# Building the gate matrices of a retrieval layer from three bf16 parts instead of two scaled fp16 parts

## The chip, the cores and the metric

The kernel runs on one core of one Trainium2 chip. The metric is device microseconds (us) of one execution. Before the change it takes 2091.34 us, the median of three runs (2091.04 to 2091.83).

Engine names below are those of the profile: PE is the matrix engine, PEld its weight loads, DVE the vector engine, ACT the scalar engine, POOL the GpSimd engine, SP the engine that issues the transfers.

## The reference, cut to what matters

The layer is a token mixer (pooling, windowed attention and cross-attention, gated and merged), followed by a product-key retrieval over 16,384 single-neuron experts, and a final normalisation. Only the retrieval is touched:

```
q = (hf @ w_q).reshape(T, 8 heads, 2, 128)
s_top, i_top = top_k(q . sub_keys, 16)          # per half: 16 of 128 keys
s_fin, pos = top_k(all 16 x 16 sums, 16)        # 16 experts for each token and head
ids = i_top[first half] * 128 + i_top[second half]
gates = softmax(s_fin)
y = sum over the 128 chosen experts: gate * gelu(x . expert_u[id]) * expert_v[id]
```

T is 512 tokens and the model width is 1024. An expert number is a pair (i, j) of numbers below 128.

## The kernel before, in words

**How the retrieval is computed.** The kernel gathers nothing. It computes all 16,384 activations for all 512 tokens, multiplies them by a gate matrix that is zero where an expert was not chosen, and multiplies the product by all expert values. The experts are cut into 128 blocks of 128: block i holds the experts (i, 0) to (i, 127).

**The stream.** All weights come as 430 chunks of 128x1024 f32, four in flight (`raw`). Each chunk is split in two: ACT rounds it to `w_hi` (line 771), POOL subtracts to get `w_lo` (line 421), and PE multiplies in three passes, high by high, high by low and low by high. `product` (line 442) is one chunk: eight pieces of the contraction times three passes, so 24 matmuls of 512 columns, all at line 448. Both `w_hi` and `w_lo` have two buffers.

**The first matrix product of the retrieval** is 128 such products, one for each block (`experts`, line 698), in three stretches of PE's program: 48 plain ones (`I_PLAIN`), 64 with gate work between them (`I_GATES`), 16 plain ones. ACT applies the gelu from the bank (line 969), and the result is stored to memory (`a_rows`).

**The gate stage** is the stretch of 64, and the change is in it. In each of its 64 steps PE first does the 24 matmuls of one block of experts, and then builds the gate matrices of 8 tokens (`TOK_I`). The gate matrix of a token is 128x128, entry (j, i), and is the product of two matrices with the token's 128 chosen experts (8 heads of 16) along the contraction: `ohJ` has a one where the expert's j is, `ohI` has the expert's gate where its i is. DVE builds both. For each step (`one_hots`, line 1333) it compares a ramp with the i numbers (`eqI`, line 1339), waits until PE is done with the buffer (line 1341), compares the ramp with the j numbers (`ohJ`, line 1342), and multiplies `eqI` by the gates (`ohI`, line 1345). Each of these works on 128x1024 elements of 16 bits. `ohJ`, `eqI` and `ohI` have two buffers each, so DVE may be up to two steps ahead of PE.

**How a gate is carried in 16 bits.** The gates are multiplied by 2^15 (`GATE_SCALE`), rounded to fp16, and the rest is rounded to fp16 again: two parts (`GATE_PARTS`). So `ohI` is made twice, and PE does two matmuls of 128 columns for each token, 16 in a step (line 729), into two banks, four tokens in each. ACT reads the banks back, multiplies by 2^-15 and writes `gstage` (line 993), which is stored to memory (`g_rows`, line 301).

**What sets the order.** Each engine's program is written out by hand and runs in order; semaphores join them. In the gate stage PE waits for `lo_ready` (POOL's half of the chunk), `proj_read` (ACT's gelu), `gate_read` (ACT's reading of the gate banks) and `hot_ready` (DVE's matrices). DVE waits for `gate_mm` (PE's gate matmuls two steps back). ACT waits for `chunk_used` and `gate_mm`; POOL waits for `hi_ready`, which ACT gives.

**Before the gate stage**, DVE finds the top experts, PE turns their i, j and gates so that experts lie on partitions (line 713), and DVE widens them into `I2`, `J2` and `G2` (lines 1320 to 1327). **After it** come the 16 plain blocks and then the value stage, which loads both stored matrices again, multiplies them on DVE (line 1364) and on PE by the expert values (line 645).

Of the kernel before, what the change touches and what calls it, by code (L numbers as in the profile page):

```python
# [18 lines left out]
T, D, P = 512, 1024, 128  # L19
# [6 lines left out]
PEER_H, TOPK, NKEYS = 8, 16, 128  # L26
# [25 lines left out]
TOK_I = T // I_GATES  # L52
# [4 lines left out]
SMALLS = 6  # L57
QUARTERED = 28
AHEAD = 6
GATE_PARTS, GATE_SCALE = 2, 2.0 ** 15  # L60


def build(nc, dram, out):
    f32, f32r, f16, u32, i32 = (mybir.dt.float32, mybir.dt.float32r, mybir.dt.float16,
                                mybir.dt.uint32, mybir.dt.int32)
    ACT, ALU, AX = mybir.ActivationFunctionType, mybir.AluOpType, mybir.AxisListType

    with ExitStack() as ctx:
# [6 lines left out]
        class Place:  # L75
# [2 lines left out]
                self.at = at  # L78

            def __call__(self, name, shape, dt=f32):  # L80
                size = int(np.prod(shape)) * (2 if dt == f16 else 4)
                line = 512 if size % 512 == 0 else 64
                at = (arena_at + self.at + line - 1) // line * line
                t = nc.alloc_sbuf_tensor_at(name, [P] + list(shape), dt, offset=at)
                self.at = at - arena_at + size
                assert self.at <= arena_size, (name, self.at)
                return t

        keep = Place(0)
# [9 lines left out]
        pscale = keep("pscale", [4])  # L99
        sinks = keep("sinks", [16])  # L100
        freq = keep("freq", [2])
        iota_b = keep("iota_b", [NKEYS], f16)
        iota_k = keep("iota_k", [TOPK])
        eps = keep("eps", [1])
        ssum = keep("ssum", [8])
# [52 lines left out]
        r = Place(front)  # L158
# [4 lines left out]
        GT = r("GT", [T])  # L163
        R1 = r("R1", [T])
        gsm = r("gsm", [TT * PEER_H])
        I2 = r("I2", [T, 2], f16)
        J2 = r("J2", [T, 2], f16)
        G2 = r("G2", [GATE_PARTS, T, 2], f16)
        eqI = r("eqI", [2, TOK_I, NKEYS], f16)
        ohJ = r("ohJ", [2, TOK_I, NKEYS], f16)  # L170
        ohI = r("ohI", [2, GATE_PARTS, TOK_I, NKEYS], f16)
        late = r.at
        sc = r("sc", [TT, 2 * PEER_H, NKEYS])
        cand = r("cand", [PEER_H, TOPK * TOPK])
# [22 lines left out]
        bank = [ctx.enter_context(nc.psum_tensor(f"bank{b}", [P, 512], f32)) for b in range(8)]  # L197
# [5 lines left out]
        def sem(name):  # L203
            return ctx.enter_context(nc.semaphore(name))
# [28 lines left out]
        spread, spread_read = sem("spread"), sem("spread_read")  # L233
        hot_ready, gate_mm, gate_read = sem("hot_ready"), sem("gate_mm"), sem("gate_read")
# [201 lines left out]
        def _(pe):  # L436
# [60 lines left out]
            for q in range(4):  # L497
                chunk(S_VM + q)
                for k in range(2):
                    for m in range(MT):  # L500
                        for low_m, w in ((0, w_hi), (0, w_lo), (1, w_hi)):
                            last = pe.matmul(bank[2 + m][:, :], memT[low_m][:, 2 * q + k, m * P:(m + 1) * P],
                                             w[:, q % 2, k * T:(k + 1) * T],
                                             start=(q == 0 and k == 0 and low_m == 0 and w is w_hi),
                                             stop=(q == 3 and k == 1 and low_m == 1))
# [78 lines left out]
            for u in range(8):  # L584
# [4 lines left out]
                for n in range(TT):  # L589
                    for h in range(2):  # L590
# [3 lines left out]
                                         start=True, stop=True)  # L594
# [7 lines left out]
            for u in range(4):  # L602
# [3 lines left out]
                for n in range(TT):  # L606
                    last = pe.matmul(mem_scores(u, n), qr[:, u % 2, n * P:(n + 1) * P], kmT[:, u, :],
                                     start=True, stop=True)
# [89 lines left out]
            def experts(i0, di):  # L698

                n, rn = S_U + di, R_U + di  # L700
                chunk(n + i0)
                pe.wait_ge(proj_read, rn - 1 + i0)
                product(bank[rn % 2][:, :], n % 2, hT)
# [14 lines left out]
            with pe.Fori(0, I_GATES - 2 + 1, 2) as i0:  # L718
                for di in range(2):
                    experts(i0 + I_PLAIN, di)  # L720
                    for b in range(2):

                        pe.wait_ge(gate_read, i0 * 2 + (2 * di + b + 1))
                        if b == 0:
                            pe.wait_ge(hot_ready, i0 + (di + 1))
                        for tk in range(TOK_I // 2):
                            at = b * (TOK_I // 2) + tk
                            for q in range(GATE_PARTS):
                                last = pe.matmul(bank[2 + b][:, tk * P:(tk + 1) * P], ohJ[:, di, at, :],  # L729
                                                 ohI[:, di, q, at, :], start=(q == 0), stop=(q == GATE_PARTS - 1))  # L730
                        last.then_inc(gate_mm, 1)
            with pe.Fori(I_PLAIN + I_GATES, NI - 1, 2) as i0:
                for di in range(2):
# [25 lines left out]
        def _(act):  # L759
            step = Steps(act, act_step)  # L760
# [25 lines left out]
            for k in range(KC):  # L786
                act.wait_ge(turned, k + 1)
                act.activation(memT_hi[:, k, :], bank[k][:, 0:M], ACT.Copy,
                               scale=gains[:, 1, k:k + 1]).then_inc(turned_hi, 1)
# [172 lines left out]
            def gelu(i0, di):  # L962
                base = S_U + di
                split(base + 2, loop=i0)
                act.wait_ge(chunk_used, base + 1 + i0)

                if not (isinstance(i0, int) and i0 + di < 2):
                    act.wait_ge(a_stored[di % 2], (i0 + (di - di % 2)) * 8)
                act.activation(abuf[:, di % 2, :], bank[(R_U + di) % 2][:, :],  # L969
                               ACT.Gelu_apprx_tanh).then_inc(proj_read, 1)  # L970
# [12 lines left out]
            def gates_out(i0, first=False):  # L983
                for half in range(2):
                    if not first:
                        act.wait_ge(g_stored[half], i0 * (4 * 16 // (2 * PER)))
                    for k in range(PER):
                        di = half * PER + k
                        gelu(i0 + I_PLAIN, di)
                        for b in range(2):  # L990
                            act.wait_ge(gate_mm, i0 * 2 + (2 * di + b + 1))
                            t0 = k * TOK_I + b * TOK_I // 2
                            act.activation(gstage[:, half, :, t0:t0 + TOK_I // 2].rearrange("p i t -> p t i"),  # L993
                                           bank[2 + b][:, :].rearrange("p (t i) -> p t i", i=NKEYS),
                                           ACT.Copy, scale=1.0 / GATE_SCALE).then_inc(gate_read, 1)

            gates_out(0, first=True)
            with act.Fori(2 * PER, I_GATES - 2 * PER + 1, 2 * PER) as i0:
                gates_out(i0)
# [30 lines left out]
        def _(dve):  # L1030
            step = Steps(dve, dve_step)
# [285 lines left out]
            def pairs(src):  # L1317
                return src.unsqueeze(2).broadcast_to([P, T, 2])

            dve.tensor_copy(I2[:, :, :], pairs(bank[2][:, :]))  # L1320
            dve.tensor_copy(J2[:, :, :], pairs(bank[3][:, :]))
            dve.tensor_scalar(G2[:, 0, :, :], pairs(bank[4][:, :]), GATE_SCALE, None, ALU.mult)
            dve.tensor_scalar(GT[:, :], bank[4][:, :], GATE_SCALE, None, ALU.mult).then_inc(spread_read, 1)
            dve.wait_ge(spread_read, 1)

            step(dve.tensor_tensor(R1[:, :], GT[:, :], G2[:, 0, :, 0], ALU.subtract))
            step(dve.tensor_copy(G2[:, 1, :, :], pairs(R1[:, :])))

            keys = [P, TOK_I, NKEYS // 2, 2]
            ramp = iota_b[:, :].rearrange("p (n e) -> p n e", e=2).unsqueeze(1).broadcast_to(keys)  # L1330
# [2 lines left out]
            def one_hots(i0, di, first=False):  # L1333
                toks = bass.ds(i0 * TOK_I + di * TOK_I, TOK_I)

                def over_keys(src):
                    return src.unsqueeze(2).broadcast_to(keys)

                dve.tensor_tensor(eqI[:, di, :, :].rearrange(wide, e=2), ramp, over_keys(I2[:, toks, :]), ALU.is_equal)
                if not first:  # L1340
                    dve.wait_ge(gate_mm, i0 * 2 + (2 * di - 2))
                dve.tensor_tensor(ohJ[:, di, :, :].rearrange(wide, e=2), ramp, over_keys(J2[:, toks, :]), ALU.is_equal)  # L1342
                dve.drain()
                for q in range(GATE_PARTS):
                    last = dve.tensor_tensor(ohI[:, di, q, :, :].rearrange(wide, e=2),  # L1345
                                             eqI[:, di, :, :].rearrange(wide, e=2),
                                             over_keys(G2[:, q, toks, :]), ALU.mult)
                last.then_inc(hot_ready, 1)

            for di in range(2):  # L1350
                one_hots(0, di, first=True)
            with dve.Fori(2, I_GATES - 2 + 1, 2) as i0:
                for di in range(2):
                    one_hots(i0, di)
# [110 lines left out]
```

## Time and profile before

| what | value |
|---|---|
| median of three runs | 2091.34 us |
| the profiled execution | 2091.04 us |
| its span, first to last instruction | 2088.5 us |
| PE busy | 2041.2 us, 98% of the span |
| PE weight loads busy | 1680.6 us, 80% |
| DVE busy | 1169.3 us, 56% |
| ACT busy | 791.9 us, 38% |
| POOL busy | 893.0 us, 43% |
| transfers | 323.46 MB, 155 GB/s over the span |

The span is what the profiler sees between the first and the last instruction; the 2.5 us between it and the execution's time lie outside the engines' programs. A row of the timeline gives a start in us from the start of the span, a duration, and in brackets the idle time of the engine ahead of it with what ended that idle time.

### The profile page before, as it was taken

The page shows a single profiled execution, that of the slowest core. Times are in us where ns is not written, and L with a number is a line of the kernel's source. Part 1 is how long each engine was busy: PE and PEld are TensorE (multiplying, and loading weights), DVE is VectorE, ACT ScalarE, POOL GpSimd, SP SyncE. Part 2 cuts the span into 40 slices and gives each one's busy share as a digit, 9 for nine tenths or more (in the row PEclk, how much of TensorE's full clock was granted, in tenths as well). Part 3 has the DMA queues.
Part 4 walks back from the last instruction along what each step waited for, and adds up shares of the span by engine and source line. Part 5 has one row for each costly group of instructions (what it writes and reads, how often), then busy time and mean ns, then how long its engine had stood idle before and what let it go on. Part 6 is the DMA issues. An engine that isn't in the chain of part 4 may idle for free.

```text
span 2088.5 us, 29235 instructions
## 1 busy us (share of the span) xinstructions
PE 2041.2 (98%) x10104; PEld 1680.6 (80%) x10104; DVE 1169.3 (56%) x1785; ACT 791.9 (38%) x1136; POOL 893.0 (43%) x445
## 2 busy tenths in 40 slices
PE   7989999999999999999999999999999999999998
PEld 6767788887888888888888888888888888888886
DVE  5677222222129999777777774035555555555556
ACT  5477423223222222355555554222223232232323
POOL 6522144443335444444444444444444444444443
PEclk9999999999999999999999999999999999999999
DMA  5211122222224445446666666764555555555552
GB/s 222 86 37 41 51 91 100 94 97 81 80 81 136 150 136 151 138 128 204 203 201 201 201 201 202 239 247 181 189 198 211 181 185 188 201 208 180 186 189 97
DMA packets 108515, 323.46 MB, mean 155 GB/s; under 512 B 11200, under 2 KB 11200, under 8 KB 106304
## 3 DMA queue, kind: packets, MB, share of 16 engines
q1 hardware_dynamic: 108192, 322.49, 45.9%
q10 hardware_dynamic: 288, 0.54, 0.1%
q8 instruction: 18, 0.29, 0.1%
q14 instruction: 17, 0.14, 0.0%
HBM read 253.78 MB, written 69.21 MB: 155 GB/s over the span
## 4 chain that ended last, share of the span: by engine, by line
issue 44%; PE 32%; POOL 22%; DMA 0%; POOLq 0%; DVE 0%; ACT 0%; SPq 0%
PE bank L645 32%; POOL w_lo L421 22%; DMA a_in<-a_rows 0%; POOLq L418 0%; DVE x_sb L1390 0%; POOLq L428 0%; DVE x_sb L1385 0%; DVE wf L1364 0%; POOL mask L405 0%; POOL mask L403 0%; DVE wT_lo L1368 0%; ACT wT_hi L1002 0%; POOL mask L400 0%; POOLq L425 0%; POOL mask L408 0%
## 5 line engine op out<-in xcount | busy, mean ns | idle before, releaser
L421 POOL TENSOR_TENSOR w_lo<-raw,w_hi 128x1024 fp32r<-128x1024 f32 (+1 forms) x430 | 889.4, 2076 | 1176.8 <-ACT w_hi L771 1176.8
L771 ACT ACTIVATE w_hi<-raw 128x1024 fp32r<-128x1024 f32 x346 | 366.7, 1060 | 1194.1 <-PE bank L448 673.8
L448 PE MATMUL bank<-hT_hi,w_hi 128*128 128x512 f32 x1488 | 591.5, 397 | 0.5 <-POOL w_lo L421 0.4
L448 PE MATMUL bank<-hT_hi,w_lo 128*128 128x512 f32 x1488 | 580.8, 390 | 0.0
L448 PE MATMUL bank<-hT_lo,w_hi 128*128 128x512 f32 x1488 | 579.6, 390 | 0.0
L1368 DVE TENSOR_TENSOR wT_lo<-wf,wT_hi 128x512 fp32r<-128x512 f32 x128 | 313.0, 2445 | 130.7 <-ACT wT_hi L1002 130.7
L448 PEld LDWEIGHTS bank<-hT_hi,w_lo 128*128 128x128 f32 x1488 | 279.5, 188 | 59.8
L448 PEld LDWEIGHTS bank<-hT_hi,w_hi 128*128 128x128 f32 x1488 | 280.0, 188 | 59.0 <-issue 4.0
L448 PEld LDWEIGHTS bank<-hT_lo,w_hi 128*128 128x128 f32 x1488 | 280.3, 188 | 56.1 <-issue 0.7
L645 PE MATMUL bank<-w_hi,wT_hi 128*128 128x512 f32 x1024 | 315.5, 389 | 0.1
L645 PE MATMUL bank<-w_lo,wT_hi 128*128 128x512 f32 x1024 | 315.4, 389 | 0.0
L645 PE MATMUL bank<-w_hi,wT_lo 128*128 128x512 f32 x1024 | 315.4, 389 | 0.0
L1364 DVE TENSOR_TENSOR wf<-a_in,g_in 128x512 f32<-128x512 f32 x128 | 88.9, 694 | 253.3 <-PE bank L645 159.5
L645 PEld LDWEIGHTS bank<-w_hi,wT_hi 128*128 128x128 f32 x1024 | 192.2, 188 | 40.3 <-DVE wT_lo L1368 0.5
L645 PEld LDWEIGHTS bank<-w_lo,wT_hi 128*128 128x128 f32 x1024 | 192.3, 188 | 39.9
L645 PEld LDWEIGHTS bank<-w_hi,wT_lo 128*128 128x128 f32 x1024 | 192.3, 188 | 39.8
L1345 DVE TENSOR_TENSOR ohI<-eqI,G 128x1024 f16<-128x1024 f16 x128 | 209.9, 1678 | 9.2
L993 ACT ACTIVATE gstage<-bank 128x512 f32<-128x512 f32 x128 | 129.7, 1123 | 0.0
L1213 DVE TENSOR_TENSOR part<-sg,bank 128x512 f32<-128x512 f32 x24 | 15.1, 683 | 171.8 <-PE bank L448 171.8
L1342 DVE TENSOR_TENSOR ohJ<-iota_b,J 128x1024 f16<-128x1024 f16 x64 | 44.3, 692 | 107.3 <-PE bank L729 107.3
L1002 ACT ACTIVATE wT_hi<-wf 128x512 fp32r<-128x512 f32 x128 | 78.6, 614 | 3.4 <-DVE wf L1364 3.2
L969 ACT ACTIVATE abuf<-bank 128x512 f32<-128x512 f32 x128 | 74.2, 580 | 1.6 <-DMA a_rows<-abuf 1.6
(215 smaller groups left out, 1462.9 us busy)
## 6 DMA issues: line engine op xcount, KB each, us to landing
raw<-stream SPq DMA_DIRECT2D x346, 512.0 KB, 3.5
a_rows<-abuf SPq DMA_DIRECT2D x128, 256.0 KB, 4.0
g_rows<-gstage SPq DMA_DIRECT2D x32, 1024.0 KB, 6.1
g_in<-g_rows SPq DMA_DIRECT2D x16, 2048.0 KB, 9.1
a_in<-a_rows SPq DMA_DIRECT2D x128, 256.0 KB, 3.5
x_sb<-x SPq DMA_DIRECT2D x4, 512.0 KB, 8.5
out<-x_sb SPq DMA_DIRECT2D x4, 512.0 KB, 2.6
subkeys<-subkeys SPq DMA_DIRECT2D x1, 1024.0 KB, 14.5
```

The source lines that it names most:

```text
L421: last = pool.tensor_tensor(w_lo[:, k % 2, cols], raw[:, k % RAW, cols], w_hi[:, k % 2, cols].bitcast(f32), ALU.subtract)
L448: last = pe.matmul(dst, w[:, slot, k * P:(k + 1) * P], rhs[low][:, r0 + k - k0, :], start=(k == k0 and wi == 0), stop=(k == k1 - 1 and wi ...
L645: last = pe.matmul(bank[2 * t + half][:, :], lhs[low_l][:, t * P:(t + 1) * P], w[:, slot, half * 512:(half + 1) * 512], start=first and lo ...
L771: act.activation(w_hi[:, base % 2, :], raw[:, slot, :], ACT.Copy).then_inc(hi_ready, 1)
L969: act.activation(abuf[:, di % 2, :], bank[(R_U + di) % 2][:, :], ACT.Gelu_apprx_tanh).then_inc(proj_read, 1)
L993: act.activation(gstage[:, half, :, t0:t0 + TOK_I // 2].rearrange("p i t -> p t i"), bank[2 + b][:, :].rearrange("p (t i) -> p t i", i=NKEYS),
L1002: act.activation(wT_hi[:, di % 2, :], wf[:, di % 2, :], ACT.Copy).then_inc(weighted_hi, 1)
L1213: dve.tensor_tensor(part[:, q, :], sg[:, q, :], bank[b][:, :], ALU.mult).then_inc(branch_read, 1)
L1342: dve.tensor_tensor(ohJ[:, di, :, :].rearrange(wide, e=2), ramp, over_keys(J2[:, toks, :]), ALU.is_equal)
L1345: last = dve.tensor_tensor(ohI[:, di, q, :, :].rearrange(wide, e=2), eqI[:, di, :, :].rearrange(wide, e=2), over_keys(G2[:, q, toks, :]), ...
L1364: dve.tensor_tensor(wf[:, di % 2, :].rearrange(tiles, b=BLOCKS), a_in[:, di % 4, :].rearrange(tiles, b=BLOCKS), g_in[:, di // GROUP, :, di ...
L1368: dve.tensor_tensor(wT_lo[:, di % 2, :], wf[:, di % 2, :], wT_hi[:, di % 2, :].bitcast(f32), ALU.subtract).then_inc(weighted_lo, 1)
```

## The change

The two scaled fp16 parts become three bf16 parts without a scale. All 16-bit tiles (`iota_b`, `I2`, `J2`, `G2`, `eqI`, `ohJ`, `ohI`) become bf16. The numbers in the comparisons are below 128, which both types hold exactly.

```
-GATE_PARTS, GATE_SCALE = 2, 2.0 ** 15
-        G2 = r("G2", [GATE_PARTS, T, 2], f16)
+        G2 = r("G2", [3, T, 2], bf16)
-        ohI = r("ohI", [2, GATE_PARTS, TOK_I, NKEYS], f16)
+        ohI = r("ohI", [2, 3, TOK_I, NKEYS], bf16)
...
-                            for q in range(GATE_PARTS):
+                            for q in range(3):
                                 last = pe.matmul(bank[2 + b][:, tk * P:(tk + 1) * P], ohJ[:, di, at, :],
-                                                 ohI[:, di, q, at, :], start=(q == 0), stop=(q == GATE_PARTS - 1))
+                                                 ohI[:, di, q, at, :], start=(q == 0), stop=(q == 2))
...
-                                           ACT.Copy, scale=1.0 / GATE_SCALE).then_inc(gate_read, 1)
+                                           ACT.Copy).then_inc(gate_read, 1)
...
-            dve.tensor_scalar(G2[:, 0, :, :], pairs(bank[4][:, :]), GATE_SCALE, None, ALU.mult)
-            dve.tensor_scalar(GT[:, :], bank[4][:, :], GATE_SCALE, None, ALU.mult).then_inc(spread_read, 1)
+            dve.tensor_copy(G2[:, 0, :, :], pairs(bank[4][:, :]))
+            dve.tensor_copy(GT[:, :], bank[4][:, :]).then_inc(spread_read, 1)
...
             step(dve.tensor_copy(G2[:, 1, :, :], pairs(R1[:, :])))
+            step(dve.tensor_tensor(GT[:, :], R1[:, :], G2[:, 1, :, 0], ALU.subtract))
+            step(dve.tensor_copy(G2[:, 2, :, :], pairs(GT[:, :])))
...
-                for q in range(GATE_PARTS):
+                for q in range(3):
                     last = dve.tensor_tensor(ohI[:, di, q, :, :].rearrange(wide, e=2),
```

In the changed program every line after 60 has a number that is one lower, up to the added DVE lines, and one higher after them. PE, in one step of the gate stage, before (bank2 and bank3 are the two gate banks, `ohI` the moving and `ohJ` the stationary operand; the first rows are the end of a block of experts):

```order
L448 MATMUL bank0<-hT_hi_50,w_lo_54 128x512
L723 ISA
L725 REGISTER_ALU [waits gate_read]
L729 MATMUL bank2<-ohI_118,ohJ_117 128x128 [waits hot_ready]
L729 MATMUL bank2<-ohI_118,ohJ_117 128x128 x7
L723 REGISTER_ALU
L729 MATMUL bank3<-ohI_118,ohJ_117 128x128 [waits gate_read]
L729 MATMUL bank3<-ohI_118,ohJ_117 128x128 x7
```

And the same place in the changed program:

```order
L447 MATMUL bank0<-hT_hi_50,w_lo_54 128x512
L722 ISA
L724 REGISTER_ALU [waits gate_read]
L728 MATMUL bank2<-ohI_118,ohJ_117 128x128 [waits hot_ready]
L728 MATMUL bank2<-ohI_118,ohJ_117 128x128 x11
L722 REGISTER_ALU
L728 MATMUL bank3<-ohI_118,ohJ_117 128x128 [waits gate_read]
L728 MATMUL bank3<-ohI_118,ohJ_117 128x128 x11
```

Each bank gets 12 matmuls where it had 8; the waits stand where they stood.

DVE, from the widening of the gates to the first matrices and the first step of the loop, before (`G_115` is `G2`, `R_111` is `R1`):

```order
L1322 TENSOR_SCALAR G_115<-bank 128x1024
L1323 TENSOR_SCALAR GT<-bank 128x512
L1326 TENSOR_TENSOR R_111<-GT,G_115 128x512 [waits spread_read]
L1327 CAST G_115<-R_111 128x1024 [waits dve_step]
L1339 TENSOR_TENSOR eqI<-iota_b,I_113 128x1024 [waits dve_step]
L1342 TENSOR_TENSOR ohJ<-iota_b,J_114 128x1024
L1345 TENSOR_TENSOR ohI<-eqI,G_115 128x1024 x2
```

And the same place in the changed program:

```order
L1321 CAST G_115<-bank 128x1024
L1322 COPY GT<-bank 128x512
L1325 TENSOR_TENSOR R_111<-GT,G_115 128x512 [waits spread_read]
L1326 CAST G_115<-R_111 128x1024 [waits dve_step]
L1327 TENSOR_TENSOR GT<-R_111,G_115 128x512 [waits dve_step]
L1328 CAST G_115<-GT 128x1024 [waits dve_step]
L1340 TENSOR_TENSOR eqI<-iota_b,I_113 128x1024 [waits dve_step]
L1343 TENSOR_TENSOR ohJ<-iota_b,J_114 128x1024
L1346 TENSOR_TENSOR ohI<-eqI,G_115 128x1024 x3
```

Two DVE instructions are added once, and one `ohI` multiplication in every step. The instructions of ACT, POOL and SP keep their order and number.

## Rows read from the trace of the kernel before

**Rows 1.** Busy time of each engine in the gate stage, one window.

```profile
core 0: us, PE busy (x) PEld busy (x) DVE busy (x) ACT busy (x) POOL busy (x), PEclk, DMA share, GB/s
887.50:1300.15 412.65, 412.65 (x2562) 338.60 (x2562) 282.71 (x247) 221.88 (x256) 179.14 (x64) 1.00 0.60 194
```

**Rows 2.** The waits of three engines in the gate stage, 885 to 1300 us.

```profile
engine line waited for: us in total, times, longest us
POOL w_lo L421 <- ACT w_hi L771: 235.4, 65, 4.0
ACT w_hi L771 <- PE bank L448: 191.6, 64, 3.9
DVE ohJ L1342 <- PE bank L729: 107.3, 62, 1.7
```

**Rows 3.** Timeline of PE, around two gate bursts, one step apart.

```profile
1003.56 1.07 PE L729 MATMUL bank<-ohI,ohJ 128*128 128x128 f16 x16
1004.44 0.47 PE L448 MATMUL bank<-hT_hi,w_hi 128*128 128x512 f32 x1
1004.75 0.39 PE L448 MATMUL bank<-hT_lo,w_hi 128*128 128x512 f32 x1
...
1010.01 1.07 PE L729 MATMUL bank<-ohI,ohJ 128*128 128x128 f16 x16
```

**Rows 4.** Timeline of ACT, two plain steps ahead of the gate stage.

```profile
848.27 1.06 ACT L771 ACTIVATE w_hi<-raw 128x1024 fp32r<-128x1024 f32 x1 [3.94 <-PE bank L448]
853.71 1.06 ACT L771 ACTIVATE w_hi<-raw 128x1024 fp32r<-128x1024 f32 x1 [3.90 <-PE bank L448]
```

**Rows 5.** The gate matmuls and their weight loads, min/median/max ns, first and last start; one burst's loads.

```profile
L729 PEld LDWEIGHTS bank<-ohI,ohJ x1024: 95/98/101, 887.5 to 1294.5; 128*128 128x128 f16 x171
L729 PE MATMUL bank<-ohI,ohJ x1024: 218/219/231, 887.5 to 1294.5; 128*128 128x128 f16 x171
...
1003.56 0.90 PEld L729 LDWEIGHTS bank<-ohI,ohJ 128*128 128x128 f16 x16 [0.26 <-issue]
```

**Rows 6.** Timeline of PE, a burst of f32 matmuls of 128 columns.

```profile
869.84 0.60 PE L713 MATMUL bank<-ident,IF 128*128 128x128 f32 x4
870.27 0.60 PE L713 MATMUL bank<-ident,JF 128*128 128x128 f32 x4
```

**Rows 7.** Timeline of DVE, one step of the gate stage (and the first of its two `ohI` alone).

```profile
1004.76 0.69 DVE L1342 TENSOR_TENSOR ohJ<-iota_b,J 128x1024 f16<-128x1024 f16 x1 [1.73 <-PE bank L729]
1005.60 3.29 DVE L1345 TENSOR_TENSOR ohI<-eqI,G 128x1024 f16<-128x1024 f16 x2
1005.60 2.68 DVE L1345 TENSOR_TENSOR ohI<-eqI,G 128x1024 f16<-128x1024 f16 x1
1008.80 0.68 DVE L1339 TENSOR_TENSOR eqI<-iota_b,I 128x1024 f16<-128x1024 f16 x1
```

**Rows 8.** Timeline of POOL, one with DVE resting beside it, one in the gate stage.

```profile
860.29 2.40 POOL L421 TENSOR_TENSOR w_lo<-raw,w_hi 128x1024 fp32r<-128x1024 f32 x1 [3.04 <-ACT w_hi L771]
1004.89 2.84 POOL L421 TENSOR_TENSOR w_lo<-raw,w_hi 128x1024 fp32r<-128x1024 f32 x1 [3.61 <-ACT w_hi L771]
```

**Rows 9.** Timeline of ACT, one step of the gate stage.

```profile
1003.76 1.06 ACT L771 ACTIVATE w_hi<-raw 128x1024 fp32r<-128x1024 f32 x1 [2.97 <-PE bank L448]
1005.20 2.02 ACT L993 ACTIVATE gstage<-bank 128x512 f32<-128x512 f32 x2
```

**Rows 10.** Timeline of DVE ahead of the gate stage.

```profile
873.62 1.21 DVE L1322 TENSOR_SCALAR G<-bank 128x1024 f16<-128x1024 f32 x1
875.47 0.69 DVE L1326 TENSOR_TENSOR R<-GT,G 128x512 f32<-128x512 f32 x1
876.19 0.69 DVE L1327 CAST G<-R 128x1024 f16<-128x1024 f32 x1
880.94 0.68 DVE L1345 TENSOR_TENSOR ohI<-eqI,G 128x1024 f16<-128x1024 f16 x1
886.35 0.68 DVE L1339 TENSOR_TENSOR eqI<-iota_b,I 128x1024 f16<-128x1024 f16 x1
```

More of the change, by code:

```diff
@@ L59 @@
 AHEAD = 6
-GATE_PARTS, GATE_SCALE = 2, 2.0 ** 15
 def build(nc, dram, out):
-    f32, f32r, f16, u32, i32 = (mybir.dt.float32, mybir.dt.float32r, mybir.dt.float16,
-                                mybir.dt.uint32, mybir.dt.int32)
+    f32, f32r, bf16, u32, i32 = (mybir.dt.float32, mybir.dt.float32r, mybir.dt.bfloat16,
+                                 mybir.dt.uint32, mybir.dt.int32)
     ACT, ALU, AX = mybir.ActivationFunctionType, mybir.AluOpType, mybir.AxisListType
@@ L80, in __call__ @@
             def __call__(self, name, shape, dt=f32):
-                size = int(np.prod(shape)) * (2 if dt == f16 else 4)
+                size = int(np.prod(shape)) * (2 if dt == bf16 else 4)
                 line = 512 if size % 512 == 0 else 64
@@ L101, in build @@
         freq = keep("freq", [2])
-        iota_b = keep("iota_b", [NKEYS], f16)
+        iota_b = keep("iota_b", [NKEYS], bf16)
         iota_k = keep("iota_k", [TOPK])
@@ L165, in build @@
         gsm = r("gsm", [TT * PEER_H])
-        I2 = r("I2", [T, 2], f16)
-        J2 = r("J2", [T, 2], f16)
-        G2 = r("G2", [GATE_PARTS, T, 2], f16)
-        eqI = r("eqI", [2, TOK_I, NKEYS], f16)
-        ohJ = r("ohJ", [2, TOK_I, NKEYS], f16)
-        ohI = r("ohI", [2, GATE_PARTS, TOK_I, NKEYS], f16)
+        I2 = r("I2", [T, 2], bf16)
+        J2 = r("J2", [T, 2], bf16)
+        G2 = r("G2", [3, T, 2], bf16)
+        eqI = r("eqI", [2, TOK_I, NKEYS], bf16)
+        ohJ = r("ohJ", [2, TOK_I, NKEYS], bf16)
+        ohI = r("ohI", [2, 3, TOK_I, NKEYS], bf16)
         late = r.at
```

## The prediction
> **What bounds the kernel now.** I read the page first (PE busy 98% of the span), then the busy time of the gate stage, which is all the change touches. There PE is busy for all 412.65 us, at a granted clock of 1.00, which is the 2.4 GHz level, while DVE works 282.71, ACT 221.88 and POOL 179.14 [rows 1]. The list of waits says the same from the other side: POOL waits for ACT, ACT waits for PE, DVE waits for PE, and PE waits for nobody [rows 2]. So PE sets the pace of the stage, and the reader should see DVE as an engine that rests 1.73 us in each step of 6.45 us until PE gives it back a buffer [rows 3, 7].
>
> One step, from burst to burst, is 1010.01 - 1003.56 = 6.45 us [rows 3]. A plain step without gate work is 853.71 - 848.27 = 5.44 us [rows 4], 24 matmuls at 0.227 us. The gate burst of 16 matmuls thus costs 1.01 us of PE's time in each of the 64 steps. Nothing ahead of PE hides any of it.
>
> **The change part by part.**
>
> *PE: 8 more matmuls of 128 columns in each of 64 steps, 512 in all.* They stand in one row with the 16 that are there, behind the same waits. What does one cost? The trace gives four readings, and they lie close together. From the first gate matmul to the first matmul of the next block, 1004.44 - 1003.56 = 0.88 us for 16 [rows 3]: 55.0 ns. The burst's own row spans 1.07 us and one matmul takes 0.219 [rows 3, 5], so 15 starts in 0.85 us: 56.7 ns. The burst's weight loads span 0.90 us at 0.098 each [rows 5]: 53.5 ns. And the whole excess of a step, 1.01 us over 16: 63 ns; this is the upper end, because it also holds what is paid once in a step and not for each matmul, such as the 0.31 us between the first two f32 matmuls behind the burst where the others take 0.227 [rows 3, 4]. I take 56 ns, between the two readings from matmul starts: 8 x 0.056 = 0.448 us in a step, 64 x 0.448 = 28.7 us. The ends are 512 x 0.0535 = 27.4 us and 512 x 0.063 = 32.3 us.
>
> That bf16 costs what fp16 costs is not shown by a row of bf16, as there is none. But a column takes 0.227/512 = 0.443 ns in the f32 passes of the product [rows 4] and 0.056/128 = 0.438 ns in the fp16 burst: in this kernel even a change of width does not change the time of a column. Each matmul loads its own stationary matrix, also where the one before used the same one (1024 loads for 1024 matmuls [rows 5]), and at 53.5 ns from start to start the loads keep up with matmuls at 56 ns. Eight more of either do not alter that.
>
> The Trainium skill, "TensorE: Matmul & The Clock Gate", section "Wait — 56ns, not 53.3ns?", has a matmul of 128 columns start every 55.6 ns at the full clock. By that figure, as an estimate, the term would be 28.5 us; the row's 55.0 and 56.7 ns lie around it.
>
> *DVE: one more `ohI` multiplication a step.* Two of them take 3.29 us, the first alone 2.68 [rows 7]. The first is long because POOL's subtraction runs beside it from 1004.89 to 1007.73 [rows 8]; it ends 0.55 us after POOL, and the second adds 3.29 - 2.68 = 0.61. Without POOL beside it one takes 0.68 [rows 10]. So the third costs 0.6 us if it runs behind POOL's, which it does: the first ends at 1008.28, POOL ended at 1007.73. DVE's chain in a step is from 1004.76 to 1009.48, 4.72 us [rows 7]; it becomes 5.3 us, in a step of 6.45 + 0.45 = 6.90 us. DVE still rests 1.6 us, and it is a step ahead of PE at that. Cost: nothing, hidden behind PE's products. If the third were also held up by POOL (2.0 us more) the chain would be 7.3 us, 0.4 over the step, or 26 us more in 64 steps; that needs a second POOL instruction inside one step, and there is one only. At the other end there is nothing to gain on DVE.
>
> One detail will move. DVE's `ohJ` waits for the end of the burst, which comes 0.45 us later, at about 1005.20 in the times of this step. POOL's subtraction is released by ACT's `w_hi`, which waits for the product and not for the burst [rows 9], and starts at 1004.89. So POOL will start first, and `ohJ` rather than the first `ohI` will be the long one: it ends 0.55 us after POOL, at about 7.84 instead of 5.45, the three `ohI` follow at about 8.0, 8.6 and 9.2, `eqI` ends at 10.5, and the next release comes at 12.1. DVE rests the same 1.6 us. POOL then should take 2.40 us as it does beside a resting DVE, not 2.84 [rows 8]. PE needs its result only when the next product is done, some 3 us after 1007.73, so neither change is worth anything.
>
> The Trainium skill, "SBUF — State Buffer", section "Who interferes with whom", says that a DVE instruction with two SBUF inputs and a GpSimd instruction that reads SBUF exclude each other, and that whoever starts first holds the port to the end. By that rule `ohJ` (start 1004.76) held up POOL and POOL held up `ohI`, as the trace has it, and the exchange just described follows. It also speaks against this change: five DVE instructions back to back can keep POOL out. By the same rows the most that POOL can lose is one DVE instruction, 0.69 us of its 3 us of cover, so the time would be the same.
>
> *DVE, once:* the two scaled conversions become plain ones, at the same element counts (1.21 us for the wide one [rows 10]); added are one subtraction and one conversion of the sorts that take 0.69 us each, 0.72 from start to start [rows 10]. With the third `ohI` the first step's matrices are ready at 881.62 + 1.44 + 0.60 = 883.7 us; PE's first burst starts at 887.5 [rows 5]. The second step's, ready at 886.4 before, come at 889.1 for a burst at about 894.4. Covered, with 3.8 and 5.3 us to spare; even a hold-up of 2.4 us by POOL fits.
>
> *ACT:* `gstage` loses its scale and keeps size and count, 2.02 us for two, ending at 1007.22, and PE's next burst is at 1010.01 [rows 3, 9]. The banks are full 0.45 us later and there are still over 2 us. Cost nothing.
>
> *SP, transfers, POOL:* same instructions, same bytes; each step is 0.45 us longer, so they have more room. The larger tiles move others in SBUF by 6 KB a partition, which has no price in any row.
>
> *Sum.* 2091.04 us for the profiled execution + 28.7 = 2119.7 us. The median before is 0.3 us above that execution, so the expected median is 2120.0 us. Single steps: 5.44 us plain, 6.90 us with gates.
>
> **The rivals.**
>
> A, *the added matmuls cost more than those before* (a longer burst drains what feeds PE). For it: the burst is the fastest run of instructions in the program, a load and a matmul every 56 ns against 227 in the product. Against: 16 pairs show no slowing, and every burst is alike (matmuls 218 to 231 ns [rows 5]). Its price, if the extra ones went at the pace of f32 matmuls of 128 columns, 0.43/4 = 108 ns [rows 6]: 512 x 0.108 = 55 us, 2146 us; anything between 2124 and that belongs to it.
>
> B, *DVE becomes the bound.* The mechanism: the bf16 instructions don't run at the 0.68 us of the fp16 ones but at the pace of a conversion of 1024 elements from the banks, 1.21 us [rows 10]. Then a step is 5 x 1.21 + 2.0 (POOL) + 0.15 = 8.2 us, against 6.90: 64 x 1.3 = 83 us on top, 2203 us. It decides from 0.95 us for each instruction (5 x 0.95 + 2.15 = 6.90). For it: the trace has no bf16 row. Against: same width, same shapes, and fp16 at 0.68 us where 512 f32 elements take 0.69 [rows 10], so what counts there is the bytes.
>
> C, *not slower: bf16 matmuls are faster than fp16 ones.* Place: the burst. 24 of them would have to fit in the 0.88 us of the 16, so 36.7 ns each; from there on the kernel is no slower, and the time stays at 2091 us. Against: both types of the kernel take 0.44 ns for a column. For it: only that no bf16 row exists. The other way to the same end, that the burst falls into idle time of PE, is excluded by the stage's PE busy time [rows 1]. A part of it would be the 0.26 us by which the weight loads rest ahead of each burst [rows 5]; if the third part let that vanish, the kernel would gain 16.6 us back, 2103 us, but the matmuls themselves show no gap there.
>
> **How the numbers follow.** The forecast, PE pays 53.5 to 63 ns for each of 512 matmuls and nothing else shows: 0.91. A: 0.04. B: 0.03. C: 0.02, half of it the case at 2103 us, which is still faster than the forecast but slower than before. The forecast's own range is 2118.7 to 2123.6; with 0.4 us for the scatter of the runs it is 2118.2 to 2124.0, and more than 9 in 10 fall there, so it needs no stretching to the other cases. 0.2% is 4.2 us, about what a measurement of this kernel tells from no change. Slower: forecast, A, B and half of C, 0.99; within it: 0.008; faster 0.002.
>
> **What the profile after would show.** Right: bursts of x24 about 1.5 us long, with the next f32 matmul 1.33 us behind the first of the burst; bursts 6.90 us apart; PE busy throughout, no wait of PE on DVE; DVE waiting 1.6 us a step at `ohJ`; a long `ohJ` (2.6 us), short `ohI` and POOL at 2.4 us. The stages ahead of 887.5 us and behind the gate stage keep their lengths. Wrong: PE waiting for `hot_ready` (B), bursts apart by more than 6.97 us with a gap inside them (A), or less than 6.87 us (C).

## The result, and the profile after

The changed kernel takes 2123.37 us, the median of four timed executions (2119.13 to 2125.07), against 2091.28 us (2091.04 to 2091.83) for the kernel before: a ratio of 1.0146, 95% interval 1.0128 to 1.0165. Forecast were 2120.0 us and 2118.2 to 2124.0. All its ten executions lie between 2118.74 and 2128.57 us, a scatter that the kernel before did not show at first. One execution of the kernel before, run beside the later experiments, took 3440.47 us at a mean granted clock of 0.556 and is left out everywhere below. The profiled execution took 2123.92 us, with a span of 2121.9.

What answers to [rows 1] and [rows 2] is one window of the gate stage from its first burst on (columns as in rows 1), and the waits in it:

```profile
892.27:1333.40 441.13, 441.13 (x3073) 367.00 (x3073) 321.25 (x313) 221.91 (x256) 154.04 (x64) 1.00 0.56 182
```

```profile
POOL w_lo L420 <- ACT w_hi L770: 292.8, 66, 4.5
ACT w_hi L770 <- PE bank L447: 223.6, 65, 3.9
DVE ohJ L1343 <- PE bank L728: 96.5, 61, 1.6
PEld bank L728 <- issue: 16.7, 64, 0.3
```

PE is busy throughout at a granted clock of 1.00, waits for nobody, and the others wait for it. A step of PE, the answer to [rows 3], and all gate matmuls, the answer to [rows 5]:

```profile
1009.46 1.51 PE L728 MATMUL bank<-ohI,ohJ 128*128 128x128 bf16 x24
1010.78 0.47 PE L447 MATMUL bank<-hT_hi,w_hi 128*128 128x512 f32 x1
1011.09 0.39 PE L447 MATMUL bank<-hT_lo,w_hi 128*128 128x512 f32 x1
```

```profile
L728 PEld LDWEIGHTS bank<-ohI,ohJ x1536: 96/98/100, 892.3 to 1327.8; 128*128 128x128 bf16 x192
L728 PE MATMUL bank<-ohI,ohJ x1536: 219/219/230, 892.3 to 1327.8; 128*128 128x128 bf16 x192
```

The next matmul starts 1.32 us behind the first of the burst, where it was 0.88, and still takes 0.47 us with 0.31 to the one after it: what is paid once in a step has not grown. The next burst starts at 1016.35 us, so a step is 6.89 us, where 6.90 were forecast. From the first gate matmul to the last are 435.5 us, and 407.0 before: 28.5 us for 512 more matmuls (504 in 63 steps and 8 in the last burst), 55.7 ns each. With the first starts, 887.5 and 892.3, and the spans the whole difference falls in three parts: 4.8 us ahead of the gate stage, 28.5 in it, 0.1 behind it (2121.9 - 1327.8 = 794.1; 2088.5 - 1294.5 = 794.0).

DVE and POOL in a step, the answers to [rows 7] and [rows 8]:

```profile
1011.10 2.63 DVE L1343 TENSOR_TENSOR ohJ<-iota_b,J 128x1024 bf16<-128x1024 bf16 x1 [1.61 <-PE bank L728]
1013.88 1.89 DVE L1346 TENSOR_TENSOR ohI<-eqI,G 128x1024 bf16<-128x1024 bf16 x3
1015.69 0.68 DVE L1340 TENSOR_TENSOR eqI<-iota_b,I 128x1024 bf16<-128x1024 bf16 x1
```

```profile
1010.79 2.40 POOL L420 TENSOR_TENSOR w_lo<-raw,w_hi 128x1024 fp32r<-128x1024 f32 x1 [4.49 <-ACT w_hi L770]
```

The exchange is there: POOL now starts 0.31 us ahead of `ohJ` and takes 2.40 us, `ohJ` takes 2.63, the three `ohI` 1.89 together, and DVE rests 1.61 us.

The 4.8 us ahead of the gate stage were not foreseen. They are what is left of a delay that arises in the windowed attention, between 120 and 220 us, in code that the change does not touch. The last scaling of that stage starts 7.9 us later than before (214.3 and 206.4 us). Part of it is won back further on: by the lines of the kernel before, DVE's first instruction of line 1213 starts 6.0 us later (276.7 and 270.7), ACT's first of line 960 4.7 us later (527.4 and 522.7). In the attention stage DVE scales the probabilities in eight rounds of eight short instructions, and in each round POOL subtracts a chunk in four pieces. The first round takes 4.07 us in both traces. The second to fourth, before:

```profile
124.64 2.66 DVE L1182 TENSOR_SCALAR prob<-prob,rinv 128x256 f32<-128x256 f32 x8
137.87 2.19 DVE L1182 TENSOR_SCALAR prob<-prob,rinv 128x256 f32<-128x256 f32 x8
151.16 2.66 DVE L1182 TENSOR_SCALAR prob<-prob,rinv 128x256 f32<-128x256 f32 x8
```

```profile
126.39 2.87 POOL L421 TENSOR_TENSOR w_lo<-raw,w_hi 128x256 fp32r<-128x256 f32 x4 [12.65 <-ACT w_hi L771]
139.67 3.04 POOL L421 TENSOR_TENSOR w_lo<-raw,w_hi 128x256 fp32r<-128x256 f32 x4 [10.41 <-ACT w_hi L771]
152.91 2.87 POOL L421 TENSOR_TENSOR w_lo<-raw,w_hi 128x256 fp32r<-128x256 f32 x4 [10.20 <-ACT w_hi L771]
```

And the same three rounds after:

```profile
125.02 3.14 DVE L1181 TENSOR_SCALAR prob<-prob,rinv 128x256 f32<-128x256 f32 x8
138.65 3.60 DVE L1181 TENSOR_SCALAR prob<-prob,rinv 128x256 f32<-128x256 f32 x8
152.74 4.07 DVE L1181 TENSOR_SCALAR prob<-prob,rinv 128x256 f32<-128x256 f32 x8
```

```profile
126.50 2.92 POOL L420 TENSOR_TENSOR w_lo<-raw,w_hi 128x256 fp32r<-128x256 f32 x4 [12.39 <-ACT w_hi L770]
139.74 3.10 POOL L420 TENSOR_TENSOR w_lo<-raw,w_hi 128x256 fp32r<-128x256 f32 x4 [10.32 <-ACT w_hi L770]
153.29 3.10 POOL L420 TENSOR_TENSOR w_lo<-raw,w_hi 128x256 fp32r<-128x256 f32 x4 [10.45 <-ACT w_hi L770]
```

In the first of these DVE starts 0.38 us later against the start of the span, POOL only 0.11, so DVE's lead on POOL is 1.48 us instead of 1.75. More of the scaling then lies beside POOL's work, and the round takes 0.48 us longer. The lead shrinks to 1.09 and 0.55 us in the next two rounds, which take 3.60 and 4.07 us, and the four behind these take 4.07 to 4.14 us each. Before, the lead stays at 1.75 to 1.80 us up to the seventh round, and a round takes 2.19 or 2.66 us; the rounds are 13.2 to 13.3 us apart there, and 13.6 and 14.1 after.

### The profile page after: what moved, and what is told of

The parts are those of the page before. It is cut to its first block, busy times and chain, and to the rows that moved or that the text cites. A ratio compares the mean times of both kernels' runs of the same rounds, so it can differ in the third digit from the quotient of the medians.

```text
span 2121.9 us, 30387 instructions
## 1 busy us (share of the span) xinstructions
PE 2068.2 (97%) x10616; PEld 1705.7 (80%) x10616; DVE 1217.6 (57%) x1851; ACT 791.6 (37%) x1136; POOL 869.7 (41%) x445
## 4 chain that ended last, share of the span: by engine, by line
issue 46%; PE 32%; POOL 21%; DMA 0%; POOLq 0%; DVE 0%; ACT 0%; SPq 0%
PE bank L644 32%; POOL w_lo L420 21%; DMA a_in<-a_rows 0%; POOLq L417 0%; DVE x_sb L1391 0%; POOLq L427 0%; DVE x_sb L1386 0%; DVE wf L1365 0%; POOL mask L402 0%; POOL mask L404 0%; DVE wT_lo L1369 0%; ACT wT_hi L1001 0%; POOL mask L399 0%; POOLq L424 0%; SPq L267 0%
## 5 line engine op out<-in xcount | busy, mean ns | idle before, releaser
L420 POOL TENSOR_TENSOR w_lo<-raw,w_hi 128x1024 fp32r<-128x1024 f32 (+1 forms) x430 | 866.1, 2022 | 1233.4 <-ACT w_hi L770 1233.4
L1343 DVE TENSOR_TENSOR ohJ<-iota_b,J 128x1024 bf16<-128x1024 bf16 x64 | 164.1, 2565 | 96.5 <-PE bank L728 96.5
L1346 DVE TENSOR_TENSOR ohI<-eqI,G 128x1024 bf16<-128x1024 bf16 x192 | 121.3, 687 | 9.2
L728 PEld LDWEIGHTS bank<-ohI,ohJ 128*128 128x128 bf16 x1536 | 85.9, 98 | 16.7 <-issue 16.7
L728 PE MATMUL bank<-ohI,ohJ 128*128 128x128 bf16 x1536 | 96.9, 219 | 0.0
```

Source lines behind the costliest of these rows:

```text
L420: last = pool.tensor_tensor(w_lo[:, k % 2, cols], raw[:, k % RAW, cols], w_hi[:, k % 2, cols].bitcast(f32), ALU.subtract)
```

## The experiments

Two theories went in. M: the change costs 512 matmuls of 55.4 ns on PE and nothing else, whatever the 16-bit type. R: the rest is the meeting of POOL and DVE in the attention stage, which comes out differently from one execution to the next, in any version. The rivals: T, the type bears part of the cost; D, DVE's third multiplication bears part of it; S, the scatter comes from the start of the program and is only carried along. A reader should know that no long execution of the kernel before was profiled; what its executions above 2096 us hold is read from traces of the variants.

The first four experiments ran on one chip, the last three on another. Beside the first four stood 23 executions of the kernel before, which themselves spread over 2090.99 to 2101.53 us, median 2097.16. So the close agreement of the first four executions of before had been the lower part of a wide spread. A median of four to twelve executions is therefore uncertain by some microseconds, and the length of the gate stage in each trace is the sharper evidence.

**Three fp16 parts (e1).** The kernel before, with the counts of the change.

```
-GATE_PARTS, GATE_SCALE = 2, 2.0 ** 15
+GATE_PARTS, GATE_SCALE = 3, 2.0 ** 15
...
             step(dve.tensor_copy(G2[:, 1, :, :], pairs(R1[:, :])))
+            step(dve.tensor_tensor(GT[:, :], R1[:, :], G2[:, 1, :, 0], ALU.subtract))
+            step(dve.tensor_copy(G2[:, 2, :, :], pairs(GT[:, :])))
```

> The kernel before with three scaled fp16 parts, so the counts of the change without its type. Theory M (the time is the 512 added matmuls at 55.4 ns each, whatever the 16-bit type): gate steps of 6.89 us, the gate stage 28.3 us longer, fastest executions at 2119.1 us as with bf16. Theory T (the type bears part of the cost): steps shorter than 6.89 us and a fastest execution clearly under 2119 us. Theory R (the executions of the changed kernel above 2119 us come from the attention stage, where POOL's and DVE's instructions meet in a different order from one execution to the next): some executions again 3 to 9 us above the fastest, and where the profile is of such a one, the extra time lies between 120 and 220 us of the span and DVE's scaling of the probabilities has a mean over 500 ns instead of 414.

Measured: 2120.16 to 2128.57 us, median 2123.83, ratio 1.0136 (1.0110 to 1.0162). The lowest of the four is 1.1 us above the 2119.1 expected. All gate matmuls:

```profile
L729 PE MATMUL bank<-ohI,ohJ x1536: 219/219/230, 893.5 to 1329.0; 128*128 128x128 f16 x192
```

First to last are 435.5 us, as with bf16. The profiled execution (2125.1 us) is one of the long ones, its first burst 6.0 us later than before, and DVE's scaling, over the whole attention stage, has this row, against 435 ns before (the 414 of the expectation is the mean without the first round):

```profile
L1182 DVE TENSOR_SCALAR prob<-prob,rinv 128x256 f32<-128x256 f32 x64 | 32.6, 581 | 0.3
```

The type bears nothing of the gate stage's cost with three parts.

**Two bf16 parts (e2).** The changed kernel without its third part.

```
-        ohI = r("ohI", [2, 3, TOK_I, NKEYS], bf16)
+        ohI = r("ohI", [2, 2, TOK_I, NKEYS], bf16)
...
-                            for q in range(3):
+                            for q in range(2):
...
-            step(dve.tensor_tensor(GT[:, :], R1[:, :], G2[:, 1, :, 0], ALU.subtract))
-            step(dve.tensor_copy(G2[:, 2, :, :], pairs(GT[:, :])))
```

> The changed kernel with two bf16 parts instead of three; it leaves out the third part of each gate, so the gates are rounded to 16 bits. Theory M: the time of the kernel before, 2091.0 to 2091.8 us in its fast executions, gate steps of 6.45 us, bursts of 16 with the next matmul 0.88 us behind the first. Theory T: between 2091 and 2119, or DVE's 16-bit instructions no longer at 0.68 us. Theory R: nothing in the gate stage, but executions some us above the fastest may occur, as with any program.

Measured: 2090.68 to 2099.41 us, median 2096.91, against 2097.16 for the kernel before beside it: ratio 0.9995 (0.9980 to 1.0010). The gate matmuls and DVE's `ohI`:

```profile
L728 PE MATMUL bank<-ohI,ohJ x1024: 219/219/230, 894.2 to 1301.2; 128*128 128x128 bf16 x171
```

```profile
L1344 DVE TENSOR_TENSOR ohI<-eqI,G 128x1024 bf16<-128x1024 bf16 x128 | 210.0, 1679 | 9.2
```

407.0 us from first to last, and 1679 ns where fp16 had 1678. T falls, from the other side too.

**PE's third matmul alone (e3).**

```
-                            for q in range(GATE_PARTS):
+                            for at_q, q in enumerate((0, 1, 1)):
                                 last = pe.matmul(bank[2 + b][:, tk * P:(tk + 1) * P], ohJ[:, di, at, :],
-                                                 ohI[:, di, q, at, :], start=(q == 0), stop=(q == GATE_PARTS - 1))
+                                                 ohI[:, di, q, at, :], start=(at_q == 0), stop=(at_q == 2))
```

> The kernel before, where PE takes the second fp16 part a second time (it adds that part twice, so the output is off in the last bits of the gates); DVE's work is as before. Theory M: the full 28.3 us, steps of 6.89 us. A rival, that part of the cost comes with DVE's third multiplication or with the larger tiles: less than 28 us here. The order of POOL and DVE in a step should already be exchanged, since it hangs on the end of the burst alone: ohJ about 2.6 us, ohI 0.68, POOL's subtraction 2.40.

Measured: 2119.51 to 2125.66 us, median 2124.30, ratio 1.0133 (1.0108 to 1.0158). DVE and POOL in one step:

```profile
1003.89 2.64 DVE L1342 TENSOR_TENSOR ohJ<-iota_b,J 128x1024 f16<-128x1024 f16 x1 [2.14 <-PE bank L729]
1006.68 1.29 DVE L1345 TENSOR_TENSOR ohI<-eqI,G 128x1024 f16<-128x1024 f16 x2
```

```profile
1003.58 2.41 POOL L421 TENSOR_TENSOR w_lo<-raw,w_hi 128x1024 fp32r<-128x1024 f32 x1 [4.42 <-ACT w_hi L771]
```

The bursts run from 892.0 to 1327.5 us, again 435.5. PE's matmuls alone bring the whole cost in the gate stage, and the later end of the burst alone makes the exchange of POOL and `ohJ`.

**DVE's third multiplication alone (e4).**

```
+        spare = r("spare", [2, TOK_I, NKEYS], f16)
...
+                last = dve.tensor_tensor(spare[:, di, :, :].rearrange(wide, e=2),
+                                         eqI[:, di, :, :].rearrange(wide, e=2),
+                                         over_keys(G2[:, 1, toks, :]), ALU.mult)
                 last.then_inc(hot_ready, 1)
```

> The kernel before, where DVE multiplies a third time into a spare tile that nobody reads; PE's work is as before. Theory M: 2091 us in the fastest executions, steps of 6.45 us, DVE's rest at ohJ down from 1.73 to about 1.1 us. The rival (DVE's third multiplication costs something): above 2092 us in the fastest executions. POOL and DVE keep their order in a step here: ohJ 0.69 us, the first ohI 2.68, POOL 2.84. Theory R: this program has the same PE and POOL programs as before; executions some us above the fastest may still occur, with the extra time between 120 and 220 us.

Measured: 2090.90 to 2099.84 us, median 2095.75, ratio 0.9994 (0.9980 to 1.0008). One step of DVE:

```profile
1003.87 0.69 DVE L1343 TENSOR_TENSOR ohJ<-iota_b,J 128x1024 f16<-128x1024 f16 x1 [1.14 <-PE bank L730]
1004.71 3.28 DVE L1346 TENSOR_TENSOR ohI<-eqI,G 128x1024 f16<-128x1024 f16 x2
1007.91 0.68 DVE L1349 TENSOR_TENSOR spare<-eqI,G 128x1024 f16<-128x1024 f16 x1
```

The rest falls from 1.73 to 1.14 us, by the 0.6 us of the forecast, and the gate stage is 407.0 us long, from 893.1 to 1300.1: the third multiplication costs nothing. D falls. This profiled execution is a long one too, and its second round in the attention stage differs from that of before in another way than the changed kernel's:

```profile
124.76 4.07 DVE L1183 TENSOR_SCALAR prob<-prob,rinv 128x256 f32<-128x256 f32 x8
125.46 2.95 POOL L422 TENSOR_TENSOR w_lo<-raw,w_hi 128x256 fp32r<-128x256 f32 x4 [11.61 <-ACT w_hi L772]
```

DVE starts only 0.12 us later than before, but POOL 0.93 us earlier. What goes with the long course is the lead between the two, here 0.70 us.

**A fourth matmul on PE (e5)**, three times the second part, as above with (0, 1, 1, 1).

> The kernel before, where PE takes the second fp16 part three times (the output is off in the last bits of the gates): 32 matmuls in a burst, 1024 more than before. Theory M, linear in the count: steps of 6.45 + 2 x 0.443 = 7.33 us, 56.7 us more than before, fastest executions at 2147.5 us. The rival, that a longer burst is fed more slowly (the third was cheap, the fourth is not): steps above 7.4 us and a gap inside the burst's row, which should be 1.96 us long.

Measured: 2148.04 to 2157.34 us, median 2152.85, ratio 1.0287 (1.0264 to 1.0310).

```profile
997.52 1.96 PE L729 MATMUL bank<-ohI,ohJ 128*128 128x128 f16 x32
...
1004.86 1.96 PE L729 MATMUL bank<-ohI,ohJ 128*128 128x128 f16 x32
```

Steps are 7.34 us; 6.45, 6.89 and 7.34 us for 16, 24 and 32 matmuls lie on a line of about 56 ns a matmul. (From the first to the last matmul are 464.2 us, 57.2 more than before for 1024 more matmuls: 55.9 ns each.) The burst is fed no more slowly when it doubles. Its profiled execution has the early first burst (887.4 us) and is the lowest time, 2148.04; the forecast was 2147.5.

**Turns in the attention stage (e6).** POOL's subtraction waits in seven of the eight rounds until DVE has scaled the probabilities, first in the kernel before. The edit also writes the last twelve of the 28 quartered subtractions out one by one, which had stood in a loop; no run has this without the wait.

```
-            with pool.Fori(0, QUARTERED - RAW + 1, RAW) as n0:
+            with pool.Fori(0, 16 - RAW + 1, RAW) as n0:
                 for k in range(RAW):
                     low(n0 + k, k, pieces=4)
+            for n in range(16, QUARTERED):
+                if 1 <= n - (S_Q + 3) <= 7:
+                    pool.wait_ge(prob_ready, 4 * (n - (S_Q + 3)))
+                low(n, n % RAW, pieces=4)
```

> The kernel before, where POOL's subtraction for seven chunks of the attention stage waits until DVE has scaled the probabilities of the step before. Theory R (the scatter is the meeting of these two): the scatter goes, all executions within about 1 us, and the level is that of the fastest before or some us lower, 2085 to 2091.5 us; DVE's scaling takes 340 to 360 ns an instruction in all its rows. The rival, that the scatter comes from the start (loads and the clock in the first 50 us) and is only carried along: the executions scatter over 2091 to 2101 us as the kernel before does beside it. A second rival: POOL's later subtraction makes PE wait for its half of the chunk, all executions above 2096 us.

Measured: 2086.57 to 2091.37 us in 12 executions, median 2089.82. Beside it the kernel before took 2091.27 to 2092.31 us nine times and 2096.4 to 2100.74 seven times. Ratio 0.9976 (0.9965 to 0.9987): this version is faster than both kernels. DVE and POOL:

```profile
124.52 2.19 DVE L1186 TENSOR_SCALAR prob<-prob,rinv 128x256 f32<-128x256 f32 x8
137.92 2.19 DVE L1186 TENSOR_SCALAR prob<-prob,rinv 128x256 f32<-128x256 f32 x8
151.16 2.19 DVE L1186 TENSOR_SCALAR prob<-prob,rinv 128x256 f32<-128x256 f32 x8
```

```profile
126.79 2.79 POOL L421 TENSOR_TENSOR w_lo<-raw,w_hi 128x256 fp32r<-128x256 f32 x4 [11.45 <-DVE prob L1186]
```

The upper group of times is gone, as R has it. But the expectation of a scatter within 1 us was wrong: 4.8 us are left. Where they come from is not shown. The eighth round has no wait and still varies (2.67 us in this trace, 3.13 in that of the next run), and other stages were not taken apart. S as the whole cause is excluded by the seven traces without the wait: their first scaling starts between 110.03 and 111.27 us, at most 1.2 us apart, and their first gate burst between 887.4 and 894.2 us.

**The same wait in the changed kernel (e7).**

> The changed kernel with the same wait on POOL. Theories M and R together: the time of the kernel before with that wait plus 28.3 us, within 0.7 us, and as little scatter. If it is apart from that sum by more than 1 us, something of the change outside the gate stage costs time.

Measured: 2117.26 to 2119.39 us, median 2118.64, ratio 1.0118 (1.0099 to 1.0136) to the kernel before. The two medians with turns are 2118.64 - 2089.82 = 28.8 us apart, expected 28.3 within 0.7. The scatter is 2.1 us, where the changed kernel had 9.8. In the two profiled executions the gate stage is 28.7 us longer (885.8 to 1321.4 us, against 887.5 to 1294.4), but starts 1.7 us earlier, so their spans are only 27.0 us apart. The close fit of the medians may therefore owe something to chance.

## Why the prediction was right, and where it was not

**PE sets the pace and pays for every added matmul.** Right. 28.7 us were forecast; the gate stage grew by 28.5. The value of 56 ns was between the readings of 55.0 and 56.7; the runs give 55.7, and 55.9 with a fourth matmul. The upper end of 63 ns rightly held what is paid once in a step. The Trainium skill, "TensorE: Matmul & The Clock Gate", section "Wait — 56ns, not 53.3ns?", states 55.6 ns: the runs agree within 0.3 ns.

**bf16 costs what fp16 does.** Right, on PE (three fp16 parts, two bf16 parts: 435.5 and 407.0 us, as with the other type) and on DVE (1679 against 1678 ns). It had been argued from the time of a column; the two runs show it. The argument itself was weaker than it read. That a change of width leaves the time of a column alone does not hold for every matmul here: those of [rows 6] take 0.43/4 = 108 ns for 128 columns, 0.84 ns a column, at a granted clock of 1.00. And that only the bytes count on DVE does not fit the cast of [rows 10], which takes 0.69 us for 1024 f32 elements, as the subtraction does for 512.

**DVE's third multiplication is hidden.** Right: 0.6 us, as forecast, a rest of 1.61 us a step with the change, and no cost alone.

**The exchange of POOL and `ohJ`.** Right in each number: 2.63, 1.89 and 2.40 us. It costs nothing in the gate stage (28.5 us for 512 matmuls is what the matmuls alone explain), and comes from PE's burst alone. The rule of the Trainium skill, "SBUF — State Buffer", section "Who interferes with whom", that of a DVE and a GpSimd instruction that need the shared port the first to start holds it, foretold who would be slow.

**The matrices ahead of the first burst.** Right:

```profile
883.12 2.76 DVE L1340 TENSOR_TENSOR eqI<-iota_b,I 128x1024 bf16<-128x1024 bf16 x1
886.56 1.89 DVE L1346 TENSOR_TENSOR ohI<-eqI,G 128x1024 bf16<-128x1024 bf16 x3
```

The first `ohI` are done at 886.56 + 1.89 = 888.45 us and the burst starts at 892.3, 3.8 us later, as forecast. POOL did hold up one instruction there (`eqI`, 2.76 us), as was allowed for, while the first long `ohI` of before is gone.

**Rivals A, B and C.** None occurred: a burst of 32 matmuls still takes 1.96 us, without a gap; PE waits for nobody in the gate stage, so DVE was never late; the type brought no gain.

**The step that failed** is one sentence: "The stages ahead of 887.5 us and behind the gate stage keep their lengths." Behind, they did; ahead, the profiled execution lost 4.8 us. The forecast took the three close executions of the kernel before that were known as its spread, and put 0.4 us into the range for it. The true spread of that kernel, seen beside the experiments, is 10.5 us: 16 of 39 executions under 2094 us, 23 from 2096 to 2102. That the median fell in the range owes something to luck: e3, with the same program on PE, had a median of 2124.30 us, just above the range's end of 2124.0, and e1 had 2123.83. The 32.1 us between the two medians of the result are likewise more than the change costs. Compared like with like the forecast is better than the medians make it look: the lowest executions are 2090.99 and 2118.74 us, 27.8 apart, and the medians of the two versions with turns 28.8.

**What stays open:** what sets DVE's lead on POOL in the second round of the attention stage. Up to there the programs of before and after differ only in the type of `iota_b` and in where tiles lie. The changed kernel's instructions start up to 0.9 us earlier between 8 and 36 us, and a steady 0.4 us later from about 49 us on; no run here took the start apart. Whether the first four executions of before all fell in the lower group by chance or by their chip is open too.

## What to carry to other kernels

Where an engine is busy through a whole stage and waits for nobody, the price of another instruction on it is the start-to-start time of its neighbours, and the trace has it; readings that include what is paid once in a step bound it from above. On the engines beside it, count the rest in a step, and ask what the later end of a burst re-orders.

Before a few microseconds are put down to a change, look for where they arise: here 4.8 of 33.4 us lay in code that was not touched, and more executions of the kernel before showed a scatter of that size in it too. A spread in a program of fixed work can come from two engines that meet now earlier and now later. Here making one of them wait was faster than letting both try, by 1.9 us even against the lower group of before (medians 2089.82 and 2091.71 us).

## What the runs showed of the hardware that was not expected

Eight short scaling instructions of DVE beside four short subtractions of POOL take 2.19 us when they are kept apart and up to 4.07 when they meet, and the loss feeds itself, as each longer round leaves a smaller lead for the next. In the seven traces without the wait, how long a round takes goes with DVE's lead on POOL at its start: 0.55 to 0.78 us of lead go with 4.07 us or a little more, 1.06 to 1.09 with 3.60 to 3.62, 1.45 and 1.48 with 3.14, and 1.69 to 1.80 with 2.66 or 2.19. The levels are 0.47 us apart. The lead in the second round tells the course of each of the seven:

| trace | lead, second round | that round | first gate burst at |
|---|---|---|---|
| before, e5 | 1.75, 1.69 us | 2.66, 2.66 us | 887.5, 887.4 us |
| after, e3 | 1.48, 1.45 us | 3.14, 3.14 us | 892.3, 892.0 us |
| e4, e1, e2 | 0.70, 0.78, 0.69 us | 4.07, 4.11, 4.07 us | 893.1, 893.5, 894.2 us |

In after and e3 a lead that is 0.3 us shorter is enough to leave the short course. That the lead decides is read from these traces; only the wait of e6 and e7, which takes the overlap away, puts it to the test. All scaling instructions of the stage, after and before:

```profile
L1181 DVE TENSOR_SCALAR prob<-prob,rinv x64: 340/354/890, 110.5 to 214.3; 128x256 f32<-128x256 f32 x64
```

```profile
L1182 DVE TENSOR_SCALAR prob<-prob,rinv x64: 341/348/822, 110.1 to 206.4; 128x256 f32<-128x256 f32 x64
```

The first row is of the changed kernel, the second of the kernel before: the medians are alike, and only the mean (560 and 435 ns), or the last start, gives the trouble away.

Repeating a stationary matrix for a third and a fourth matmul in a row brings no saving in this program: it is loaded again each time (1536 loads for 1536 matmuls, and 2048 for 2048), and each added pair of load and matmul costs 55.7 to 55.9 ns.
